# Layer 0 expert gate and up products as pairs of 64-column weight halves, in a two-layer diffusion backbone

## The reference, cut to what matters

```
cap = CAPACITY_FACTOR * N // N_EXPERTS          # 128 of 1024 latent, 32 of 256 context
xg = jax.vmap(lambda hb, ib: hb[ib])(h, top_idx)
a = jnp.einsum('becd,edf->becf', xg, w_gate)    # D_MODEL 1024 -> EXPERT_FF 1024
u = jnp.einsum('becd,edf->becf', xg, w_up)
y = jnp.einsum('becf,efd->becd', jax.nn.silu(a) * u, w_down) * top_aff[..., None]
```

## Time and profile before

| quantity | value |
|---|---|
| median of three runs | 4283.85 us |
| the profiled execution's own time | 4276.98 us |
| its span | 4275.3 us |
| TensorE matmul busy | 4070.3 us, 95% of the span |
| TensorE weight load busy | 2868.4 us, 67% |
| VectorE busy | 1885.1 us, 44% |
| ScalarE busy | 1060.3 us, 25% |
| GpSimd busy | 251.3 us, 6% |
| chain that ended last, TensorE's part | 83% |
| mean granted TensorE clock | 0.978 of full speed |

### The profile page before, as it was taken

How to read it: one execution, slowest core, us unless ns; L and a number is a source line. 1 busy time by engine, 2 the same in 40 slices (tenths; PEclk the granted TensorE clock), 3 DMA queues, 4 the chain that set the end, 5 groups by cost and what they waited for, 6 DMA issues and landing times.

```text
span 4275.3 us, 80180 instructions
## 1 busy us (share of the span) xinstructions
PE 4070.3 (95%) x31758; PEld 2868.4 (67%) x31758; DVE 1885.1 (44%) x4141; ACT 1060.3 (25%) x2431; POOL 251.3 (6%) x262
## 2 busy tenths in 40 slices
PE   8999999999999799999998999999999987999995
PEld 4555667655544588888886555667644446899994
DVE  2235566532235443333334444666533355444444
ACT  1225555400012111111112323555410120110101
POOL 0000000000000011111111000000000000101012
PEclk9999999999999899999999999999999998999997
DMA  6111000222235798888886221000211437999995
GB/s 209 51 55 45 16 16 16 84 85 82 75 133 193 272 285 268 267 262 265 268 267 188 73 78 39 16 16 15 70 45 44 151 116 231 328 332 327 329 332 166
DMA packets 567747, 653.18 MB, mean 153 GB/s; under 512 B 20244, under 2 KB 495012, under 8 KB 567544
## 3 DMA queue, kind: packets, MB, share of 16 engines
q1 hardware_dynamic: 548600, 605.26, 44.0%
q0 software_dynamic: 18944, 45.11, 4.4%
HBM read 579.46 MB, written 70.86 MB: 152 GB/s over the span
## 4 chain that ended last, share of the span: by engine, by line
PE 83%; DVE 3%; DMA 1%; issue 1%; DVEq 1%; SPq 1%; ACT 0%; POOL 0%; POOLq 0%; ACTq 0%
PE PS L685 34%; PE PS L1169 10%; PE PS L1196 9%; PE PS L689 7%; PE PS L845 7%; PE PS L1015 5%; PE PS L903 3%; PE PS L896 2%; PE PS L823 2%; PE PS L1190 1%; DVE arena L1533 1%; PE PS L909 1%; PE PS L700 1%; DMA arena<-in_w_exp_down 1%; SPq L386 1%
## 5 line engine op out<-in xcount | busy, mean ns | idle before, releaser
L685 PE MATMUL PS<-arena 128*128 128x160 f32 (+4 forms) x7200 | 1774.7, 409 | 14.8 <-DVE arena L1533 6.4
L685 PEld LDWEIGHTS PS<-arena 128*128 128x128 f32 x7200 | 1145.6, 191 | 617.7 <-issue 559.6
L1533 DVE TENSOR_TENSOR arena<-arena,PS 128x256 f32<-128x256 f32 (+3 forms) x668 | 293.7, 448 | 1063.0 <-ACT arena L1506 563.5
L1533 DVE TENSOR_TENSOR arena<-arena 128x1024 f32<-128x1024 f32 (+9 forms) x814 | 586.4, 737 | 357.3 <-PE PS L685 234.1
L689 PEld LDWEIGHTS PS<-arena 128*128 128x128 f32 (+1 forms) x3074 | 368.0, 141 | 287.0 <-issue 200.4
L689 PE MATMUL PS<-arena 128*128 128x128 f32 (+1 forms) x3074 | 469.8, 279 | 41.8 <-DVE arena L1533 13.2
L1169 PE MATMUL PS<-arena 128*64 128x128 f32 x8192 | 452.7, 273 | 2.3 <-ACT arena L1492 1.5
L1169 PEld LDWEIGHTS PS<-arena 128*64 128x64 f32 x8192 | 451.1, 138 | 4.4 <-ACT arena L1492 1.9
L1196 PE MATMUL PS<-arena 128*64 128x256 f32 x3584 | 393.8, 380 | 1.2 <-issue 0.7
L845 PE MATMUL PS<-arena 96*128 96x512 f32 (+1 forms) x800 | 362.7, 536 | 15.0 <-issue 13.1
L1506 ACT ACTIVATE arena<-PS 128x160 f32<-128x160 f32 (+1 forms) x256 | 74.3, 290 | 1199.8 <-PE PS L685 655.9
(11 more groups left out here) (203 smaller groups left out, 2249.6 us busy)
## 6 DMA issues: line engine op xcount, KB each, us to landing
arena<-in_w_exp_gate SPq DMA_DIRECT2D x128, 1024.0 KB, 6.6
arena<-in_w_exp_up SPq DMA_DIRECT2D x128, 1024.0 KB, 9.1
arena<-in_w_exp_down SPq DMA_DIRECT2D x128, 1024.0 KB, 7.6
arena<-in_w_ada SPq DMA_DIRECT2D x24, 2048.0 KB, 16.8
arena<-in_w_in SPq DMA_DIRECT2D x32, 512.0 KB, 5.4
h_transposed<-arena SPq DMA_DIRECT2D x20, 512.0 KB, 4.4
x_mid<-arena SPq DMA_DIRECT2D x18, 512.0 KB, 2.9
moe_sum<-arena SPq DMA_DIRECT2D x18, 512.0 KB, 3.4
```

The source lines that it names most:

```text
L685: m = pe.matmul(o, lt, rh, start=start and i == 0, stop=stop and i == n - 1)
L1533: return dve.tensor_tensor(o, x, y, op)
```

## The change

```diff
@@ -1161,9 +1161,6 @@
                             pe.wait_ge(*s("act", e * 9 + f - 1))
                         for h in range(2):
                             w = ring[:, (f // 2) * 2 + h, :, (f % 2) * P:(f % 2 + 1) * P]
-                            if l == 0:
-                                m = mms(PS[:, 3 + f % 2, h * N:(h + 1) * N], [(w[:, k, :], xgT[:, k, 0:N]) for k in range(KD)])
-                                continue
                             for k in range(KD):
                                 for g in range(2):
                                     m = pe.matmul(PS[g * 64:(g + 1) * 64, 3 + f % 2, h * N:(h + 1) * N], w[:, k, g * 64:(g + 1) * 64], xgT[:, k, 0:N],
```

## The result

| | before | after |
|---|---|---|
| median of six runs each | 4283.86 us (4279.83 to 4286.64) | 4296.12 us (4294.56 to 4301.39) |
| ratio | | 1.0033, 95% interval 1.0022 to 1.0043 |
| profiled execution | 4276.98 us | 4296.14 us |
| span | 4275.3 us | 4294.4 us |

The changed kernel was 12.3 us slower in this comparison, where the forecast was 4283.8 us and no change. The profiled execution of the kernel before is not one of the six; it was made at another time. The spans lie 19.1 us apart, but 7.7 us of that is there before the first changed product starts (1471.56 us before, 1479.22 us after), and has to do with the single execution. The expert stage of layer 0, from its first gate product to the start of the last expert's down products, took 827.1 us before (1471.56 to 2298.66) and 835.9 us after (1479.22 to 2315.14).

The account below looks back on a forecast made before the run. TensorE's instruction list was taken to bound the kernel. Pitch +0.4 us, edges -0.5 us and expert 0 at 0 gave -0.1 us, so 4283.8 us against 4283.85 us, range 4279.5 to 4290.5 us.

Parts of the forecast that it names:

- The bound of the stage: Layer 0's expert stage: TensorE never waits from expert 1 on, so each microsecond on its list is one of kernel time.
- The pair's cost at 160 columns: Layer 0's gate and up products: a pair of halves costs 136.3 ns against 136.2 ns full-width, +0.4 us in all.
- rival 3: Halves don't run fully side by side at 160 columns: 4288.9 to 4300 us, or 4842 us if wholly serial; chance 0.03.
- sign of being wrong: The forecast is wrong if the pair's pitch leaves 135.5 to 137.0 ns or a turn's seam shows idle time.
- The edges: Tile-width changes around layer 0's gate and up products: down products up to -2.1 us, transposes +1.6 us, together -0.5 us.
- Expert 0: Layer 0's first expert, with waits and a low clock at its head: taken as 0, up to 2.2 us either way.
- Hidden by nothing is only TensorE's own list: Layer 0's expert stage: other engines, DMA and clock were checked, and only TensorE's list was taken to show in the time.
- the pitch term: Time of 4096 pairs of halves against full-width records in layer 0: +0.4 us, bounds -0.8 to +0.4 us.
- Rival 1: Layer 0's loop body of 1408 records is no longer kept on the core: some 36 us more, 4320 us; chance 0.07.
- Rival 2: The 2.9 ns per record beyond the columns' 133.3 ns disappears with halves: 11.9 us faster, 4272 us; chance 0.02.

Follow-up runs that it names:

- e5: The changed kernel run again without edit, on chip 5: 4298.66 us against 4285.00 us for the kernel before, ratio 1.0032.
- e8: The changed kernel run a third time without edit, on chip 1: 4281.17 us against 4280.25 us for the kernel before, ratio 1.0000.
- e3: The changed kernel with block f = 1 of layer 0's gate and up products in full-width records again: 4287.80 us, ratio 1.0016.
- e4: The kernel before with only block f = 1 of layer 0's gate and up products in halves: 4288.12 us, ratio 1.0011.
- e7: The changed kernel with only layer 0's scatters put off to the fourth block, gather left in place, chip 5: 4282.19 us, ratio 0.9996.
- e6: The kernel before with GpSimd's gather and scatters of layer 0 put off to the fourth block, chip 5: 4280.67 us, ratio 0.9993.

## Why the prediction was wrong, point by point

**The bound of the stage: right.** TensorE's list sets the length; what its streams lost came out as time (12.4 us of holes against 12.3 us measured, 13.9 against 13.7 in e5), within the few microseconds by which executions differ.

**The pair's cost at 160 columns: right where nothing disturbs it.** I forecast 136.0 to 136.3 ns. On the chips without the marker (1, 8 and 9) the stream is 34.87 us for 256 pairs, 136.2 ns, the full tile's own figure, and the changed kernel's ratio is 1.0000 (0.9990 to 1.0010) in e8. The half records really run side by side at this shape, and rival 3 is refuted, although the first comparison's 4296.12 us lies where the prediction looked for it (4288.9 to 4300 us). With the hole in it a stream of 35.32 to 35.95 us is 138.0 to 140.4 ns a pair, outside the 135.5 to 137.0 ns that the prediction had set as its sign of being wrong.

**The edges: right to 0.1 us a turn.** The down products gave back 0.09 us (12.23 to 12.14), the transposes cost 0.05 us more (0.97 to 1.03 or 1.02), and the turn without holes went from 52.27 to 52.24 us, the 0.5 us in 16 turns that was forecast. Inside a stream a width change costs more than the 0.1 us that the prediction gave each (0.17 to 0.18 us, e3 and e4), which didn't matter here, since the number of changes stayed.

**Expert 0: within its 2.2 us in kind, wider in size.** Its stream with its waits took 41.75 us before and 38.98 us after, and between 37.5 and 44.0 us in the other traces. It is where much of the spread between executions of one kernel lies.

**"Hidden by nothing is only TensorE's own list": the step that failed.** In weighing who else is touched I asked whether other engines would be slowed by TensorE and whether the clock and the DMA share allow halves, and took layer 1's undisturbed streams for the answer. I did not ask what else reaches into the stream at its head, where GpSimd issues five indirect transfers between 3.4 and 11.3 us, and what TensorE has queued to ride over an interruption; the sum had no term for either. What the runs showed in its place: on chip 5 these early scatters cost the halves 13.9 us and late ones nothing (e5 and e7), and full tiles at most 7 us (e6). In two comparisons (the first, whose chip has no number, and that on chip 5) each such stream lost 0.5 to 1.2 us there. The bounds of the pitch term, -0.8 to +0.4 us, came from rows without an interruption, and the real upper end on such a chip was +12 to +14 us. In the traces of the kernel before with the transfers in their old place the same GpSimd instructions stand beside full tiles and cost nothing, but all of these are without the marker.

Why halves suffer more is argued from the traces and not shown. What halves change is the reserve. In e8 the record of the register instruction ahead of block 2's wait stands 7.36 us into the stream, and the block's first matmul record runs at 128 x 68 ns = 8.7 us: 1.3 us of work are queued. In the kernel before it is 6.37 us against 64 x 136 ns = 8.7 us, that is 2.3 us. The number of queued records is about the same and each is worth half the time. In layer 1 it is 5.92 us against 7.0 us, or 1.1 us. The hole begins 1.1 to 1.5 us after the start of the first scatter behind the gather in layer 0 and 1.3 us after it in layer 1, about the time that is queued, as if the handing out stopped when that scatter starts.

The sizes don't close, though. In the first comparison the instruction came 1.8 us late in ten of the 13 streams in the loop, which lost 0.8 to 1.1 us, and 1.0 to 1.1 us late in the other three, which lost 0.5 to 0.8 us; in layer 1 it came 0.3 to 0.4 us late and 0.08 us were lost. A single pause shorter than the reserve should cost nothing, so lateness at this one instruction isn't the length of the pause, and that 2.3 us would ride over it is a guess. No trace of the full-width kernel with the marker and the scatters in their old place exists.

**Rival 1, the loop body: refuted.** From 1660 to 2200 us the trace after has no row of an instruction queue, only these (packets, MB, share).

```profile
q1 hardware_dynamic: 127218, 128.27, 73.5%
q0 software_dynamic: 6240, 13.11, 10.5%
```

The body of 1408 records is kept like the 1264 of layer 1, and there is no 2.8 us wait at a turn: the next row starts right behind L1193 (2066.70 above). The rival's price had a slip as well: TensorE does have work queued across a turn, for the record of the branch at L378 stands 2.1 us before the stream starts in the kernel before. Runtime: NRT & Kernel Launch in the Trainium skill, section Instruction fetch mechanics, gives TensorE 2048 instructions. The trace agrees for this body.

**Rival 2, the leftover of 2.9 ns: refuted,** by 136.2 ns a pair.

**The chances.** The time came out slower for a reason that none of the rivals named. I had counted 0.10 for slower, 0.07 of it for rival 1 and 0.03 for rival 3. The forecast of no change is what chip 1 shows, and it is false in the first comparison and on chip 5; a range that held both would have had to reach to 4299 us. That chip 1 bears the forecast out is in part luck, since nothing in the prediction tells the two kinds of chip apart.

**What stays open.** Why some chips make the pause and others don't, with the same program and the same GpSimd instructions at the same place. Why the scatters 18.6 us into the stream make no hole and no late register instruction in e7. What in the early scatters does it, the down weights' loads beside them, the gather ahead of them or something else. And whether full tiles hide the same pause.

## What to carry to other kernels

Halving each matmul while keeping the total also cut the time that TensorE's queued work is worth, here from 2.3 to 1.3 us, so beside the cost of a pair, look for what other engines do inside the stream and compare their pauses with the time queued. Transfers that nobody is waiting for, like these scatters, may stand later in a stream: on the chip where it mattered this took the changed kernel from 13.7 us over the kernel before to no difference. Before explaining a difference of a few tenths of a per cent, run both unchanged kernels once more, and look in the trace for a stretch that nobody edited: if it has changed too, the chip or the occasion is part of the cause.

## What the runs showed of the hardware that was not expected

- One and the same kernel was 13.7 us (ratio 1.0032, 1.0019 to 1.0044) over the kernel before on one chip and equal to it on another (1.0000, 0.9990 to 1.0010), each time against runs of the kernel before on that chip. One occasion on each doesn't tell the chip from the occasion.
- On chip 5 the place of GpSimd's scatters decided it: 4298.66 us with them 6 us into the stream, 4282.19 us with them 18.6 us into it.
- The granted clock was 1.00 in the stretches of 2 us with the hole as well as beside it, so the hole is not the clock.
- A change between tile widths of 64 and 128 columns inside a stream costs 0.17 to 0.18 us (0.34 us for two in e3, 0.36 us in e4). The Trainium skill, TensorEngine Tiling (Array Packing), section Key Properties, says that a change of tiling mode drains TensorE. The traces agree in that each change costs time, and give the size.
- Half-width pairs cost the same as a full-width record at 160 columns to within 0.1 ns: 34.87 us for 256 of either.
